# The branch and output projections of an encoder layer, ordered by weights over all three token chunks, with two sets of three banks

## The chip, the cores and the metric

The kernel runs on one core of one Trainium2 chip. The metric is the device time of one execution in microseconds (us).

## The reference

One encoder layer is applied to two groups of tokens, 1024 of `x_sample` and 256 of `x_prompt`, with the same weights and a model width of 1024. Cut to what the change touches:

```
y_a    = o_a   @ w_branch_a          # o_a: 1024 wide (gated linear attention)
y_b    = o_att @ w_branch_b          # o_att: 512 wide (dilated attention)
merged = sigmoid(gate_a) * y_a + sigmoid(gate_b) * y_b
x      = x + merged @ w_out
x      = x + relu(rms_norm(x) @ w_mlp1)**2 @ w_mlp2
x      = x + sigmoid(rms_norm(x) @ w_ple_gate) * (p @ w_ple_proj)
```

Everything before `y_a` (the projection by `w_in` and both attention branches) takes the first half of the kernel and is not changed.

## The kernel before

Activations lie transposed: 128 features on the partitions, 1280 tokens in the free dimension. The tokens are cut into three **chunks** of 512, 512 and 256 (`CHUNKS`, L63), one bank of the matmul accumulator each (a bank holds 512 fp32 values per partition, and there are eight). The precision of fp32 is kept by splitting both operands into a high and a low part, and a product of two tiles is three matmuls (`steps`, L690 to L701): high weights by high activations (L698), high weights by low activations (L699), low weights by high activations (L700). The high parts are made by ScalarE (a copy to the reduced type), the low parts by VectorE (a subtraction).

A **slab** is 128 output features for all tokens. Its weights, KT = 8 tiles of 128 x 128, come by one DMA of SyncE's queue into `w_raw` (`load`), are split by ScalarE (`split_high`, L1029 to L1032) and VectorE (`split_low`, L1373 to L1376, which increments `w_split`) and lie in one of two slots. TensorE computes a slab in `whole` (L703 to L709): for each chunk it waits for the weights and for the chunk's bank to have been read (`ready`, L684 to L688, which asks `evac` for chunk c of the slab before), then for inputs, and runs the 24 products of that chunk (12 where the contraction is only 512 wide), the last of which increments `mm_done`. So a slab uses banks 0, 1 and 2, chunk 0 is complete after two fifths of the slab, and the reader of a bank works while TensorE fills the next.

The change touches two stages. Stage **C1** (L924 to L927) makes `merged`, in eight rounds j of two slabs: slab A (`act_hi`, `act_lo` by `w_branch_a`, 3 x 24 products) and slab B (`ob_hi`, `ob_lo` by `w_branch_b`, 3 x 12 products). Its parts:

- Before it, in the last slab of the input projection, ScalarE evacuates a chunk (L1248) and turns that chunk of the loaded `o_a` into `act_hi` (L1253), VectorE makes `act_lo` (L1641) and increments `c_low`. Chunk c may be overwritten as soon as TensorE is through with it. TensorE's first slab waits for `c_low` per chunk.
- GpSimd waits for all of `merged` of round j-1 (`m_done`, L650) and then loads the two gate rows of round j into rows 16 and 17 of `work` (L653). ScalarE splits the weights of slab B, applies the sigmoid to both rows (L1265), and splits the weights of the next slab A (L1260 to L1266).
- VectorE (`merge_tile`, L1656 to L1675) splits the weights of slab B, waits for the sigmoid (`g_sig`), multiplies the three chunks of slab A into gate row 16 (L1669), splits the weights of the next slab A, and then per chunk of slab B multiplies into row 17 (L1669) and adds both into `merged` (L1673, which increments `m_done`).
- In the last round `merged` must also be split into `act_hi` and `act_lo` for the next stage. ScalarE does it chunk after chunk, eight rows each (L1268 to L1272), the eighth row of a chunk only after VectorE has merged that chunk; VectorE does seven rows of a chunk (L1653), then merges the chunk, then does the eighth, and increments `m_low`. Both engines go through the chunks in this one order.

Stage **C2** (L937 to L949) makes `x + merged @ w_out` in eight slabs. Per chunk TensorE waits for the bank, for `m_low` of that chunk and, at chunk 0, for the rows of x (`xn_loaded`), adds x by products with the identity (L947, ten of 128 columns per slab, each of which shows as two instructions in the trace), then runs the 24 products. ScalarE evacuates the three chunks (L1284), squares the row (L1288), and at the start of the next turn splits weights; VectorE adds up the squares (L1689) and increments `x1_acc`. When the last slab is through, ScalarE and VectorE prepare the inputs of the MLP (`norm_rows`, L1294 and L1695), and column sums of the squares (L933) give the norm.

The MLP stage (L955 to L970), which is not changed, runs `whole` for its first product and for its second one a loop over four banks (3 to 6), with six products into each before it goes to the next.

Of the kernel before, what the change touches and what calls it, by code (L numbers as in the profile page):

```python
# [19 lines left out]
ALU = mybir.AluOpType  # L20
ACT = mybir.ActivationFunctionType
# [4 lines left out]
P = 128  # L26
# [27 lines left out]
def encoder(nc, a, out_p, out_s):  # L54
# [3 lines left out]
    KT = D // P  # L58
# [29 lines left out]
    def slab_chunks(n):  # L88

        return 3 * n  # L90

    with ExitStack() as ctx:
# [590 lines left out]
        def _(pe):  # L683
# [19 lines left out]
            def whole(n, slot, kt, hi, lo, inputs=None):  # L703

                for c in range(3):
                    ready(n, c)
                    if inputs is not None:
                        inputs(c)
                    steps(slot, c, 0, kt, kt, hi, lo).then_inc(mm_done, 1)  # L709


            def transposed_x(c):

                for k in range(KT):
                    q = c * KT + k
                    if k == 0:
                        pe.wait_ge(x_norm, X_TILES[c][1])
                    if q >= 5:
                        pe.wait_ge(x_low, q - 4)
                    for i, t in enumerate(range(*X_TILES[c])):  # L720
                        mm = nc.tensor.transpose(bank[3 + q % 5][:, i * P:i * P + P], x_in[:, t, k * P:k * P + P],
                                                 ident[:])
                    mm.then_inc(x_tr, 1)
# [197 lines left out]
                whole(N_REST + j, (N_REST + j) % 2, KT, act_hi, act_lo)  # L921


            with pe.Fori(0, KT) as j:  # L924
                n = N_C1 + 2 * j
                whole(n, N_C1 % 2, KT, act_hi, act_lo, lambda c: pe.wait_ge(c_low, 8 * c + 9))
                whole(n + 1, (N_C1 + 1) % 2, 4, ob_hi, ob_lo, lambda c: pe.wait_ge(c_low, 24 + 5))  # L927


            def column_sums(row, first, last):  # L930
# [6 lines left out]
            with pe.Fori(0, KT // 2) as i:  # L937
                for e in range(2):
                    n = N_C2 + e + 2 * i
                    xt = x_row(e).rearrange("p (n d) -> p n d", d=P)  # L940
                    for c, (t0, tw) in enumerate(CHUNKS):
                        ready(n, c)
                        pe.wait_ge(m_low, 8 * c + 9)
                        if c == 0:
                            pe.wait_ge(xn_loaded[e], 32 * i + 32)
                        for q in range(tw // P):
                            nc.tensor.matmul(bank[c][:, q * P:q * P + P], xt[:, t0 // P + q, :], ident[:],  # L947
                                             start=q == 0, stop=False, skip_group_check=True)
                        steps((N_C2 + e) % 2, c, 0, KT, KT, act_hi, act_lo, first=False).then_inc(mm_done, 1)  # L949
            pe.wait_ge(head_done, H + 1)  # L950
            pe.wait_ge(x1_acc, KT + 2)
            column_sums(8, True, True).then_inc(x1_ss, 1)

# [71 lines left out]
        def _(act):  # L1025
# [250 lines left out]
            with act.Fori(0, KT // 2) as i:  # L1276
                for e in range(2):
                    n = N_C2 + e + 2 * i
                    split_high(n + 1, (N_C2 + e + 1) % 2)
                    row = work[:, bass.ds(2 * i + e, 1), :].rearrange("p o t -> p (o t)")  # L1280
                    for c, (t0, tw) in enumerate(CHUNKS):
                        act.wait_ge(mm_done, slab_chunks(n) + c + 2)
                        act.sem_inc(act_passed, 1)
                        A(row[:, t0:t0 + tw], bank[c][:, 0:tw], ACT.Copy).then_inc(evac, 1)  # L1284
                    act.wait_ge(evac, slab_chunks(n + 1) + 1)
                    act.wait_ge(x1_acc, 2 * i + e + 1)
                    act.sem_inc(act_passed, 1)
                    A(work[:, 12 + e, :], row, ACT.Square).then_inc(x1_sq, 1)  # L1288
# [80 lines left out]
        def _(dve):  # L1369
# [286 lines left out]
            def merge_tile(j, last):  # L1656
                n = N_C1 + 2 * j
                split_low(n + 1, (N_C1 + 1) % 2, 512)
                for e in range(2):
                    if e == 1:  # L1660
                        split_low(n + 2, N_C1 % 2)
                    dve.wait_ge(g_sig, 2 * j + e + 2)
                    for c, (t0, tw) in enumerate(CHUNKS):
                        if last and e == 1:
                            for k in range(KT - 1):
                                merged_low(c, k)
                        gate = work[:, 16 + e, t0:t0 + tw]
                        chunk_done(n + e, c)
                        v_.tensor_tensor(gate, bank[c][:, 0:tw], gate, ALU.mult).then_inc(evac, 1)  # L1669
                        if e == 1:  # L1670
                            dve.wait_ge(evac, slab_chunks(n + 1) + c + 2)
                            both = merged[:, bass.ds(j, 1), t0:t0 + tw].rearrange("p o t -> p (o t)")
                            v_.tensor_tensor(both, work[:, 16, t0:t0 + tw], gate, ALU.add).then_inc(m_done, 1)  # L1673
                            if last:
                                merged_low(c, KT - 1)  # L1675
# [111 lines left out]
```

## Time and profile before

| | |
|---|---|
| median of 3 runs | 2964.9 us (2960.98, 2964.90, 2965.68) |
| span of the profiled execution | 2963.3 us, from the first to the last instruction |
| time of the profiled execution outside its span | not recorded; the median run is 1.6 us above that span |
| TensorE busy | 2850.8 us (96%), 15390 matmuls and as many weight loads |
| VectorE, ScalarE, GpSimd busy | 1181.4, 991.7, 157.5 us |
| mean granted TensorE clock | 0.982 of full |
| stage C1 in the trace | 1571.9 to 1745.2 us |
| stage C2 in the trace | 1748.0 to 1878.2 us |
| MLP in the trace | 1887.3 to about 2772 us |

Times in the rows are microseconds from the span's start. "PE" is TensorE's matmul, "PEld" its weight load, "DVE" VectorE, "ACT" ScalarE, "POOL" GpSimd. Matmuls overlap in the records: what a product costs is the distance from one start to the next, not its duration. A bracket at the end of a row is the engine's idle time before it and who ended it.

### The profile page before, as it was taken

The numbers are of one execution on the slowest core, as the hardware profiler recorded it, in microseconds if no ns is written. First come the engines' busy times: TensorE is split into PE (matmuls) and PEld (weight loads), VectorE is DVE, ScalarE is ACT, GpSimd is POOL, SyncE is SP. The second block draws the span as 40 slices with busy tenths as digits, with TensorE's granted clock in tenths as the row PEclk, the third lists the DMA queues.
The fourth block names the chain that finished last, engine by engine and source line by source line (L and its number), as shares of the span: only waits on it lengthen the run. The fifth ranks groups of instructions, "written<-read, shape, count | busy, mean of one in ns | idle before, by whom it ended". The sixth has DMA issues, their size and how long they took to land.

```text
span 2963.3 us, 41636 instructions
## 1 busy us (share of the span) xinstructions
PE 2850.8 (96%) x15390; PEld 2433.3 (82%) x15390; DVE 1181.4 (40%) x1917; ACT 991.7 (33%) x1639; POOL 157.5 (5%) x247
## 2 busy tenths in 40 slices
PE   5999999999999899998999999999999999999798
PEld 5887888878888788887887888788888888888687
DVE  3224433334323443235324341454444444544533
ACT  4454225442344423544234332412112112212422
POOL 2001000010000100001010001000000000000000
PEclk8999999989999999999999999999999999999999
DMA  3122121131212211122143222111111111111022
GB/s 95 29 30 43 45 72 31 23 56 31 74 29 30 50 41 64 30 30 59 38 181 119 88 93 73 54 35 42 36 35 42 35 41 37 35 42 35 9 74 59
DMA packets 176579, 153.25 MB, mean 52 GB/s; under 512 B 13745, under 2 KB 155393, under 8 KB 176449
## 3 DMA queue, kind: packets, MB, share of 16 engines
q1 hardware_dynamic: 153824, 94.38, 11.4%
q0 software_dynamic: 16352, 57.00, 7.2%
q8 instruction: 80, 1.31, 0.2%
q10 hardware_dynamic: 6272, 0.15, 0.1%
q14 instruction: 51, 0.41, 0.1%
HBM read 127.48 MB, written 23.78 MB: 51 GB/s over the span
## 4 chain that ended last, share of the span: by engine, by line
PE 87%; DVE 4%; DMA 3%; issue 3%; ACT 2%; POOL 1%; ACTq 0%; DVEq 0%; SPq 0%; POOLq 0%
PE bank L698 25%; PE bank L700 24%; PE bank L699 24%; PE bank L857 2%; PE bank L806 2%; PE bank L787 1%; PE bank L900 1%; PE bank L882 1%; DMA stat_scratch<-st_t 1%; PE bank L897 1%; DMA work<-weight_scratch 1%; DVE work L1524 1%; PE bank L797 1%; PE bank L947 1%; DVE work L1504 1%
## 5 line engine op out<-in xcount | busy, mean ns | idle before, releaser
L698 PE MATMUL bank<-act_hi,w_hi 128*128 128x512 f32 (+1 forms) x3192 | 1189.4, 373 | 47.6 <-ACT work L1232 32.9
L700 PE MATMUL bank<-act_hi,w_lo 128*128 128x512 f32 (+1 forms) x3192 | 1139.0, 357 | 0.0
L699 PE MATMUL bank<-act_lo,w_hi 128*128 128x512 f32 (+1 forms) x3192 | 1138.5, 357 | 0.0
L698 PEld LDWEIGHTS bank<-act_hi,w_hi 128*128 128x128 f32 x3192 | 608.4, 191 | 134.7 <-ACT work L1232 35.2
L700 PEld LDWEIGHTS bank<-act_hi,w_lo 128*128 128x128 f32 x3192 | 607.0, 190 | 89.0
L699 PEld LDWEIGHTS bank<-act_lo,w_hi 128*128 128x128 f32 x3192 | 609.6, 191 | 74.4
L1032 ACT ACTIVATE w_hi<-w_raw 128x1024 fp32r<-128x1024 f32 (+2 forms) x179 | 180.0, 1006 | 437.5 <-PE bank L700 392.3
L1375 DVE TENSOR_TENSOR w_lo<-w_raw,w_hi 128x1024 fp32r<-128x1024 f32 (+2 forms) x181 | 210.8, 1165 | 242.7 <-ACT w_hi L1032 238.0
L698 PE MATMUL bank<-u_hi,w_hi 128*128 128x512 f32 (+1 forms) x816 | 289.6, 355 | 2.4 <-DVE work L1746 2.4
L699 PE MATMUL bank<-u_lo,w_hi 128*128 128x512 f32 (+1 forms) x816 | 289.5, 355 | 0.0
L700 PE MATMUL bank<-u_hi,w_lo 128*128 128x512 f32 (+1 forms) x816 | 289.0, 354 | 0.0
L1723 DVE TENSOR_TENSOR work<-bank,work 128x512 f32<-128x512 f32 (+1 forms) x384 | 226.7, 601 | 136.9 <-PE bank L700 134.0
L1232 ACT ACTIVATE work<-bank 128x512 f32<-128x512 f32 (+1 forms) x216 | 111.8, 524 | 413.5 <-PE bank L700 412.6
L698 PEld LDWEIGHTS bank<-u_hi,w_hi 128*128 128x128 f32 x816 | 154.7, 190 | 24.6 <-DVE w_lo L1375 2.8
L699 PEld LDWEIGHTS bank<-u_lo,w_hi 128*128 128x128 f32 x816 | 154.7, 190 | 21.4
L700 PEld LDWEIGHTS bank<-u_hi,w_lo 128*128 128x128 f32 x816 | 154.5, 189 | 21.6
L1315 ACT ACTIVATE utmp<-utmp 128x512 f32<-128x512 f32 (+1 forms) x96 | 53.8, 561 | 308.8 <-DVE utmp L1711 308.8
L1711 DVE SCALAR_TENSOR_TENSOR utmp<-bank,r_bc 128x512 f32<-128x512 f32 (+1 forms) x96 | 57.8, 602 | 161.5 <-PE bank L700 157.5
L1714 DVE TENSOR_TENSOR u_lo<-utmp,u_hi 128x512 fp32r<-128x512 f32 (+1 forms) x96 | 57.9, 603 | 117.0 <-ACT u_hi L1317 117.0
L1175 ACT ACTIVATE kdn<-bank 128x256 f32<-128x256 f32 x40 | 15.4, 384 | 232.4 <-PE bank L859 232.4
L561 POOL DMA_DIRECT2D stat_scratch<-st_t x48 | 49.4, 1034 | 758.9 <-DVE st_t L1475 725.0
L1442 DVE SCALAR_TENSOR_TENSOR work<-work,g_k 128x1280 f32<-128x1280 f32 x12 | 18.6, 1551 | 148.6 <-ACT work L1111 148.6
(228 smaller groups left out, 2691.7 us busy)
## 6 DMA issues: line engine op xcount, KB each, us to landing
w_raw<-in_w_in_dram SPq DMA_DIRECT2D x76, 512.0 KB, 3.7
w_raw<-in_w_mlp_dram SPq DMA_DIRECT2D x64, 512.0 KB, 3.9
gate_scratch<-work POOLq DMA_DIRECT2D x16, 640.0 KB, 3.2
work<-gate_scratch POOLq DMA_DIRECT2D x16, 640.0 KB, 6.5
work<-weight_scratch POOLq DMA_DIRECT2D x12, 640.0 KB, 5.9
oa_scratch<-work POOLq DMA_DIRECT2D x8, 640.0 KB, 6.0
work<-oa_scratch POOLq DMA_DIRECT2D x8, 640.0 KB, 8.0
x_in<-in_x_sample_dram SPq DMA_DIRECT2D x8, 512.0 KB, 8.0
```

The lines of the kernel that those rows point to most:

```text
L698: nc.tensor.matmul(out, wh, rh, start=first and k == 0, stop=False, skip_group_check=True)
L699: nc.tensor.matmul(out, wh, rl, start=False, stop=False, skip_group_check=True)
L700: mm = nc.tensor.matmul(out, wl, rh, start=False, stop=k == kt - 1, skip_group_check=True)
L806: mm = nc.tensor.matmul(bank[6][:, 0:P], ar[p0:p1, 2, m * P:m * P + P], prt[p0:p1, b % 2, i * P:i * P + P], start=i == 0, stop=i == len(pc ...
L857: nc.tensor.matmul(out, keys_, queries_, start=True, stop=True, skip_group_check=True)
L1032: A(w_hi[:, slot, 0:width], w_raw[:, 0:width], ACT.Copy).then_inc(w_high, 1)
L1232: A(dst, src, ACT.Copy, scale=DK ** -0.5 if tt == 9 else 1.0).then_inc(evac, 1)
L1315: A(buf, buf, ACT.Square).then_inc(u_sq, 1)
L1375: v_.tensor_tensor(w_lo[:, slot, 0:width], w_raw[:, 0:width], w_hi[:, slot, 0:width].bitcast(F32), ALU.subtract).then_inc(w_split, 1)
L1711: v_.scalar_tensor_tensor(out=buf, in0=bank[c][:, 0:tw], scalar=0.0, in1=r_bc[:, t0:t0 + tw], op0=ALU.max, op1=ALU.mult).then_inc(evac, 1)
L1714: v_.tensor_tensor(u_lo[:, e, t0:t0 + tw], buf, u_hi[:, e, t0:t0 + tw].bitcast(F32), ALU.subtract).then_inc(u_low, 1)
L1723: v_.tensor_tensor(x, bank[3 + jt][:, 0:tw], x, ALU.add).then_inc(w2_read if jt < 3 else evac, 1)
```

## The change

`swept` replaces `whole` in stages C1 and C2. It takes the bank set e (banks 0 to 2 or 3 to 5), waits at the slab's start for the weights and for the inputs and banks of all three chunks, and then runs the products with the chunk as the innermost loop: for each of the KT tiles and each of the three pairs of parts, the same 128 x 128 weights for chunks 0, 1 and 2. The number of products, and of weight loads that the program asks for, is the same. The wait for a bank now asks for chunk c of the slab before the last. In C2 the products with the identity for all three chunks come at the slab's start. The last product of each chunk, which increments `mm_done`, is now among the slab's last three. Two waits are added ahead of C1: for the evacuation of all earlier slabs, and for `head_done`, which stood behind C2. The readers (L1284 and L1669) take the bank of the set.

```
--- before.py
+++ after.py
@@ -707,6 +707,26 @@
                     if inputs is not None:
                         inputs(c)
                     steps(slot, c, 0, kt, kt, hi, lo).then_inc(mm_done, 1)
+
+
+            def swept(n, e, slot, kt, hi, lo, inputs, begin=None):
+
+                banks = bank[3 * e:3 * e + 3]
+                pe.wait_ge(w_split, n + 2)
+                for c in range(3):
+                    pe.wait_ge(evac, slab_chunks(n - 2) + c + 2)
+                    inputs(c)
+                    if begin is not None:
+                        begin(c, banks[c])
+                for k in range(kt):
+                    wh, wl = w_hi[:, slot, k * P:k * P + P], w_lo[:, slot, k * P:k * P + P]
+                    for w, x in ((wh, hi), (wh, lo), (wl, hi)):
+                        for c, (t0, tw) in enumerate(CHUNKS):
+                            mm = nc.tensor.matmul(banks[c][:, 0:tw], w, x[:, k, t0:t0 + tw],
+                                                  start=begin is None and k == 0 and w is wh and x is hi,
+                                                  stop=k == kt - 1 and w is wl, skip_group_check=True)
+                            if k == kt - 1 and w is wl:
+                                mm.then_inc(mm_done, 1)
 
 
             def transposed_x(c):
@@ -921,10 +941,12 @@
                 whole(N_REST + j, (N_REST + j) % 2, KT, act_hi, act_lo)
 
 
+            pe.wait_ge(evac, slab_chunks(N_C1) + 1)
+            pe.wait_ge(head_done, H + 1)
             with pe.Fori(0, KT) as j:
                 n = N_C1 + 2 * j
-                whole(n, N_C1 % 2, KT, act_hi, act_lo, lambda c: pe.wait_ge(c_low, 8 * c + 9))
-                whole(n + 1, (N_C1 + 1) % 2, 4, ob_hi, ob_lo, lambda c: pe.wait_ge(c_low, 24 + 5))
+                swept(n, 0, N_C1 % 2, KT, act_hi, act_lo, lambda c: pe.wait_ge(c_low, 8 * c + 9))
+                swept(n + 1, 1, (N_C1 + 1) % 2, 4, ob_hi, ob_lo, lambda c: pe.wait_ge(c_low, 24 + 5))
 
 
             def column_sums(row, first, last):
@@ -938,16 +960,19 @@
                 for e in range(2):
                     n = N_C2 + e + 2 * i
                     xt = x_row(e).rearrange("p (n d) -> p n d", d=P)
-                    for c, (t0, tw) in enumerate(CHUNKS):
-                        ready(n, c)
+
+                    def inputs(c):
                         pe.wait_ge(m_low, 8 * c + 9)
                         if c == 0:
                             pe.wait_ge(xn_loaded[e], 32 * i + 32)
+
+                    def residual(c, out):
+                        t0, tw = CHUNKS[c]
                         for q in range(tw // P):
-                            nc.tensor.matmul(bank[c][:, q * P:q * P + P], xt[:, t0 // P + q, :], ident[:],
+                            nc.tensor.matmul(out[:, q * P:q * P + P], xt[:, t0 // P + q, :], ident[:],
                                              start=q == 0, stop=False, skip_group_check=True)
-                        steps((N_C2 + e) % 2, c, 0, KT, KT, act_hi, act_lo, first=False).then_inc(mm_done, 1)
-            pe.wait_ge(head_done, H + 1)
+
+                    swept(n, e, (N_C2 + e) % 2, KT, act_hi, act_lo, inputs, residual)
             pe.wait_ge(x1_acc, KT + 2)
             column_sums(8, True, True).then_inc(x1_ss, 1)
 
@@ -1281,7 +1306,7 @@
                     for c, (t0, tw) in enumerate(CHUNKS):
                         act.wait_ge(mm_done, slab_chunks(n) + c + 2)
                         act.sem_inc(act_passed, 1)
-                        A(row[:, t0:t0 + tw], bank[c][:, 0:tw], ACT.Copy).then_inc(evac, 1)
+                        A(row[:, t0:t0 + tw], bank[3 * e + c][:, 0:tw], ACT.Copy).then_inc(evac, 1)
                     act.wait_ge(evac, slab_chunks(n + 1) + 1)
                     act.wait_ge(x1_acc, 2 * i + e + 1)
                     act.sem_inc(act_passed, 1)
@@ -1666,7 +1691,7 @@
                                 merged_low(c, k)
                         gate = work[:, 16 + e, t0:t0 + tw]
                         chunk_done(n + e, c)
-                        v_.tensor_tensor(gate, bank[c][:, 0:tw], gate, ALU.mult).then_inc(evac, 1)
+                        v_.tensor_tensor(gate, bank[3 * e + c][:, 0:tw], gate, ALU.mult).then_inc(evac, 1)
                         if e == 1:
                             dve.wait_ge(evac, slab_chunks(n + 1) + c + 2)
                             both = merged[:, bass.ds(j, 1), t0:t0 + tw].rearrange("p o t -> p (o t)")
```

## Rows read from the trace of the kernel before

**Rows 1.** The page's head.
```profile
span 2963.3 us, 41636 instructions
```

**Rows 2.** Busy time by stretch: us, PE, PEld, DVE, ACT, POOL; PEclk, DMA share, GB/s.
```profile
1599.50:1724.70 125.20, 125.20 (x659) 108.09 (x658) 43.92 (x68) 40.17 (x36) 6.38 (x12) 1.00 0.31 101
...
1920.00:2750.00 830.00, 830.00 (x4336) 715.79 (x4335) 394.50 (x604) 161.25 (x240) 0.00 (x0) 1.00 0.13 39
```

**Rows 3.** What TensorE waited for, 1550 to 1920 us: us, times, longest.
```profile
PE bank L698 <- DVE work L1669: 5.5, 1, 5.5
PE bank L933 <- DVE work L1689: 3.8, 1, 3.8
PE bank L947 <- DVE act_lo L1653: 2.6, 1, 2.6
```

**Rows 4.** The groups by line and form, one of the weight loads.
```profile
L699 PEld LDWEIGHTS bank<-act_lo,w_hi 128*128 128x128 f32 x3192 | 609.6, 191 | 74.4
```

**Rows 5.** Timeline of PE, two slabs: start, duration, engine, line, operation, count.
```profile
1558.16 0.40 PE L698 MATMUL bank<-act_hi,w_hi 128*128 128x512 f32 x1
...
1569.06 0.28 PE L698 MATMUL bank<-act_hi,w_hi 128*128 128x256 f32 x1
...
1571.94 0.40 PE L698 MATMUL bank<-act_hi,w_hi 128*128 128x512 f32 x1
...
1600.48 0.40 PE L698 MATMUL bank<-act_hi,w_hi 128*128 128x512 f32 x1
...
1600.94 0.39 PE L700 MATMUL bank<-act_hi,w_lo 128*128 128x512 f32 x1
```

**Rows 6.** Timeline, start of C1 and the first slab B.
```profile
1570.41 7.59 DVE L1641 TENSOR_TENSOR act_lo<-work,act_hi 128x512 fp32r<-128x512 f32 x16 [0.53 <-ACT act_hi L1253]
...
1585.60 0.28 PE L700 MATMUL bank<-act_hi,w_lo 128*128 128x256 f32 x1
...
1591.34 0.80 PE L698 MATMUL bank<-ob_hi,w_hi 128*128 128x512 f32 x1 [5.47 <-DVE work L1669]
...
1596.08 0.39 PE L700 MATMUL bank<-ob_hi,w_lo 128*128 128x512 f32 x1
```

**Rows 7.** Timeline, end of round 6 of C1 and the sigmoid of round 7.
```profile
1723.32 0.69 DVE L1669 TENSOR_TENSOR work<-bank,work 128x512 f32<-128x512 f32 x1 [1.08 <-PE bank L700]
...
1724.56 0.40 PE L698 MATMUL bank<-act_hi,w_hi 128*128 128x512 f32 x1
...
1724.77 0.41 DVE L1669 TENSOR_TENSOR work<-bank,work 128x256 f32<-128x256 f32 x1
1725.32 0.42 DVE L1673 TENSOR_TENSOR work<-work 128x256 f32 x1
...
1734.02 2.44 ACT L1265 ACTIVATE work<-work 128x1280 f32<-128x1280 f32 x2 [7.33 <-DMA work<-gate_scratch]
```

**Rows 8.** Timeline, the passage from C1 to C2 and C2's first two slabs.
```profile
1739.63 1.23 DVE L1375 TENSOR_TENSOR w_lo<-w_raw,w_hi 128x1024 fp32r<-128x1024 f32 x1 [0.67 <-ACT w_hi L1032]
...
1745.12 0.28 PE L700 MATMUL bank<-ob_hi,w_lo 128*128 128x256 f32 x1
...
1748.03 1.15 PE L947 MATMUL bank<-ident,x_next 128*128 128x128 f32 x8 [2.63 <-DVE act_lo L1653]
...
1758.33 0.42 DVE L1653 TENSOR_TENSOR act_lo<-work,act_hi 128x256 fp32r<-128x256 f32 x1 [0.48 <-ACT act_hi L1272]
...
1765.74 1.06 PE L947 MATMUL bank<-ident,work 128*128 128x128 f32 x8
...
1781.78 0.61 PE L947 MATMUL bank<-ident,x_next 128*128 128x128 f32 x4
```

**Rows 9.** Timeline of ACT, the end of C2.
```profile
1875.10 0.60 ACT L1284 ACTIVATE work<-bank 128x512 f32 x1 [5.75 <-PE bank L700]
1878.42 0.38 ACT L1284 ACTIVATE work<-bank 128x256 f32 x1 [2.72 <-PE bank L700]
...
1880.17 13.10 ACT L1294 ACTIVATE act_hi<-work,g_mlp 128x512 fp32r<-128x512 f32 x24
```

## The prediction

> **What bounds the kernel now.** I read the page's head for the span [rows 1], then the busy time by stretch [rows 2], then TensorE's list of waits around the two stages [rows 3], and last the timeline at each border. The stretches show that TensorE is the bound: inside stage C1 it is busy for all of 125.2 us at a granted clock of 1.00, while DVE works 43.9 and ACT 40.2 us [rows 2]. So a change there can pay in two ways only: a product must become cheaper, or one of TensorE's few waits must go. The list holds 5.5, 3.8 and 2.6 us [rows 3], each once.
>
> A product's price is the distance between starts. 48 products of 512 columns took 1558.16 to 1569.06, 0.2271 us each, and the next 24 of 256 columns 2.88 us, 0.120 us each [rows 5]. The difference, 0.107 us for 256 columns, is the streaming at the 2.4 GHz level; 0.013 us per product is fixed. Slab A is then 48 x 0.227 + 24 x 0.120 = 13.78 us, slab B 6.89, a round 20.67. A slab of C2 takes 16.04 (1765.74 to 1781.78) [rows 8].
>
> **Does the order by weights make a product cheaper?** I take no gain. The program before already repeats weights: L699 uses the weights of L698, and yet has its own load, 3192 of them at 191 ns [rows 4], and 0.227 us is the mean over all three lines, with no room for one of them to be 0.013 cheaper unless another is dearer. The loads lie beside the products. Nor does changing the bank show a price or a gain: the 24 products of 256 columns from 1569.06 include the step into bank 0 at 1571.94 [rows 5], and the MLP stage, which changes bank every six products, is busy for all of 830 us [rows 2].
>
> The Trainium skill (TensorE: Matmul & The Clock Gate, Step-by-step: what each phase is for) says that weights are loaded apart so that they can be loaded once and used for many products. By that the order would save the loads; no row here shows a load that is left out.
>
> What the new order does add is a step from 256 back to 512 columns in every group of three. Nearest rows: the first two products of 512 after a run of 256 took 1600.48 to 1600.94, 0.46 where two of 0.227 make 0.454 [rows 5]. That is 0.006 us per group, with the rounding 0 to 0.016. Groups: 8 rounds x 36 + 8 slabs x 24 = 480. I take +2.9 us, ends 0 and +7.7. The identity products of C2 only move together; the count is the same, and I cost that at nothing.
>
> **Start of C1.** Now all of `act_lo` must be there before the first product. VectorE ends it at 1570.41 + 7.59 = 1578.00 [rows 6]; with 0.2 us from a finish to its reader (TensorE through at 1724.56, VectorE starts 1724.77 [rows 7]) TensorE starts at 1578.2 instead of 1571.94: +6.26. The second set of banks takes away one wait: slab B of round 0 stood from 1585.60 + 0.12 = 1585.72 to 1591.34 for the late gates, 5.62 us [rows 6]. Slab B now needs banks 3 to 5, which are free, so -5.62, and slab A's banks are wanted only a slab later. TensorE was slow after that stand: 1591.34 to 1596.08 for 11 products, 4.74 against 2.50, a loss of 2.24 us [rows 6]. The new stand is as long, so the loss moves with it. Net **+0.64**, and C1 ends at 1745.24 + 0.64 = 1745.88.
>
> **Rounds of C1.** All three chunks of slab B now end together, so VectorE's merge comes behind the slab: pairs of 1.45, 1.45 and 0.97 us (1723.32 to 1724.77, and 1724.77 to 1725.32 + 0.42 [rows 7]), 3.87 with 0.21 ahead. `merged` is done 4.1 us after slab B where it was 1725.74 - 1724.56 = 1.2. GpSimd's gate load and ACT's sigmoid are queued behind it: the sigmoid starts 8.28 us after `merged` (1725.74 to 1734.02) and takes 2.44. Then come ACT's and VectorE's weight splits, 1.1 and 1.2 us. Sum 4.1 + 8.28 + 2.44 + 1.1 + 1.2 = 17.1 us into a round in which the next slab A starts at 20.67. So 3.5 us are left, and I cost this at nothing. The cover is slab B; without it each round would lose what is over.
>
> **From C1 to C2, the main term.** Before, TensorE worked on chunks 1 and 2 of the last slab and then on chunk 0 of C2 while ScalarE and VectorE split `merged` chunk by chunk; it stood only 2.63 us, and the last low part was done at 1758.33 + 0.42 = 1758.75, hidden under C2's first slab [rows 8]. Now the first slab's products need all of it. The chain also starts later. Round 6 ends at 1724.56 + 0.64 = 1725.2, `merged` is done 4.1 later (1729.3), the sigmoid starts at 1737.6 and ends at 1740.0, and the low weights follow 1.1 later, at 1741.1, where they came at 1739.63. From there to the last low part it was 19.12 us of ScalarE and VectorE in a fixed order, which I keep: 1760.2. With 0.2 to wake and 0.45 for chunk 2's identity products (a quarter of 8 + 8 + 4 instructions, the others run during the wait), the products start at 1760.9. The engine has stood for most of 14 us, so I add 2.24 for the slow clock (as after 5.6 us; the first slab of before lost 1765.74 - 1748.03 - 16.04 = 1.67; ends 1.7 and 3.4). The slab ends at 1760.9 + 13.78 + 2.24 = 1776.9, where before it was 1765.74. That is **+11.2**, the 0.64 within it.
>
> **C2 and its end.** The banks of the slab before the last are always free, the rows of x and the weights are asked for after a whole slab as before, with 16 us for them: nothing. At the end ScalarE finds three chunks to evacuate where one was left (1878.42; a copy of 512 takes 0.60 [rows 9]). Two more, back to back, are **+1.15**, and the square, the 13.10 us of `act_hi` for the MLP and all behind it follow ScalarE [rows 9]. The MLP itself is as it was.
>
> **Sum.** 11.2 + 1.15 + 2.9 = +15.2 us on the profiled span of 2963.3, so 2978.5; on the median of the runs, 1.6 above that span, 2980.1, or 0.5% slower. About 0.2%, 6 us, is what a measurement of this kernel can tell from no change.
>
> **Rivals.** (1) *The fixed 0.013 us goes.* It could be the price of writing the same bank twice running, or of changing weights. `swept` never writes a bank twice running: 1440 products x 0.0129 = 18.6 us against 12.35 of stalls and evacuation, -6.2: 2958.7. If only products whose weights repeat gain (7 of 9, 1120), it is 14.4: 2962.8. It decides from 8.6 ns per product on. Against it stand the equal spacings across a change of bank and on L699 [rows 4, 5]; for it, only that no row has both at every product. Chance 0.07, half of it faster. (2) *The clock falls in the interleaved slabs.* A product at the low level cost 2.24 / 11 = 0.204 us more [rows 6]; one in ten of 1440 would be 29 us: 3009. Against: granted 1.00 through 830 us of changing banks [rows 2]. Chance 0.03.
>
> The Trainium skill has a rule that speaks for this rival (TensorE: Matmul & The Clock Gate, A second HAM failure mode: psum-queue depth-cycling): cycling through banks lets TensorE idle in small gaps often enough that its clock goes up and down. In the MLP stage of this trace that doesn't happen.
>
> (3) *The gates come too late in C1*, with 3.5 us left. If each load were 5.5 us slower beside the weights' load, seven rounds would lose 2 each: +14, 2994. The margin speaks against it. Chance 0.04. (4) *The passage is cheaper than I read*, ScalarE and VectorE being done sooner because nothing else holds them: half the term, 2974 to 2971. Chance 0.06.
>
> **Numbers.** My own case has 0.80, and 2973 to 2987 by its ends: groups of three -2.9 to +4.8, the clock -0.5 to +1.2, the chain 1.5 either way, the runs' spread 2.5 either way. The range that leaves out no more than two in ten takes in rival 4 and some of rival 1: 2969 to 2988. Within 0.2% I put 0.08 (half of rival 1, some of rival 4), faster 0.04, slower 0.88.
>
> **What would show it.** TensorE's first C1 product near 1578 and no stand at slab B of round 0; then a stand ahead of C2's products of some 14 us, broken only by the first sixteen identity instructions, released by L1653; groups of three every 0.574 to 0.59 us; three evacuations back to back behind each slab of C2; as many weight loads as before, 15390. It would be wrong if the groups took under 0.56 us, if TensorE waited in the rounds of C1, or if the stand ahead of C2 were under 8 us.

## Result and profile after

The changed kernel takes 2983.16 us in the median of 4 runs (2982.60 to 2986.05) where the kernel before took 2965.29 (2960.98 to 2971.72): a ratio of 1.0061, 95% interval 1.0046 to 1.0075, +17.9 us. The forecast was 2980.1, in a range of 2969 to 2988, slower with a chance of 0.88. The sign and the mechanism were as forecast; one term of the sum was put at half of what it measured.

The head of the page and TensorE's list of waits from 1550 to 1920 us (us in total, times, longest), which answer to [rows 1] and [rows 3]:

```profile
span 2984.3 us, 41636 instructions
```
```profile
PE bank L972 <- DVE act_lo L1678: 10.8, 3, 5.7
PE bank L725 <- DVE act_lo L1666: 6.0, 1, 6.0
PE bank L955 <- DVE work L1714: 4.3, 1, 4.3
```

The wait for late gates (5.5 us) is gone, 6.0 us ahead of C1 and 10.8 us ahead of C2 have come (L725 is the product in `swept`, L972 the identity product, L1666 and L1678 the low parts). The timeline of TensorE at the start of C1, against [rows 6]; x3 is one group of three products:

```profile
1574.67 0.28 PE L700 MATMUL bank<-act_hi,w_lo 128*128 128x256 f32 x1
1580.99 1.41 PE L725 MATMUL bank<-act_hi,w_hi 128*128 128x512 f32 x3 [6.05 <-DVE act_lo L1666]
...
1586.96 0.74 PE L725 MATMUL bank<-act_hi,w_hi 128*128 128x512 f32 x3
```

TensorE stands (waits, without work) from 1574.67 + 0.12 to 1580.99, 6.20 us. The six groups that follow take 5.97 us where six at full clock take 3.52: 2.45 us for the 1.2 GHz level. The granted clock bears it out (busy time by stretch, columns as in [rows 2]; the clock is the third number from the end):

```profile
1581.00:1586.00 5.00, 5.00 (x14) 4.13 (x15) 3.69 (x3) 4.97 (x5) 2.74 (x4) 0.50 0.53 156
1750.00:1780.00 30.00, 19.24 (x91) 16.18 (x90) 16.67 (x30) 9.37 (x20) 1.61 (x2) 0.77 0.19 55
```

The second row holds the passage to C2, with a granted clock of 0.77 on the mean. Then the groups inside C1, against [rows 5], and the passage to C2, against [rows 8] (two engines' timelines):

```profile
1639.75 0.75 PE L725 MATMUL bank<-ob_hi,w_hi 128*128 128x512 f32 x3
...
1641.51 0.75 PE L725 MATMUL bank<-ob_hi,w_hi 128*128 128x512 f32 x3
...
1751.81 0.74 PE L725 MATMUL bank<-ob_hi,w_lo 128*128 128x512 f32 x3
1755.64 1.15 PE L972 MATMUL bank<-ident,x_next 128*128 128x128 f32 x8 [3.09 <-DVE act_lo L1678]
1762.47 2.05 PE L972 MATMUL bank<-ident,x_next 128*128 128x128 f32 x8 [5.67 <-DVE act_lo L1678]
1766.51 1.19 PE L972 MATMUL bank<-ident,x_next 128*128 128x128 f32 x4 [2.00 <-DVE act_lo L1678]
1767.36 1.20 PE L725 MATMUL bank<-act_hi,w_hi 128*128 128x512 f32 x2
...
1782.98 1.28 PE L972 MATMUL bank<-ident,work 128*128 128x128 f32 x10
```
```profile
1734.67 0.42 DVE L1698 TENSOR_TENSOR work<-work 128x256 f32 x1
...
1747.24 1.23 DVE L1400 TENSOR_TENSOR w_lo<-w_raw,w_hi 128x1024 fp32r<-128x1024 f32 x1 [0.36 <-ACT w_hi L1057]
...
1765.94 0.43 DVE L1678 TENSOR_TENSOR act_lo<-work,act_hi 128x256 fp32r<-128x256 f32 x1 [0.48 <-ACT act_hi L1297]
```

Three groups take 1.76 us, 0.587 each, where three products of the kernel before take 0.574. The last slab of C1 ends at 1752.4 and the first products of C2 come at 1767.36: 15 us, broken only by the identity products, and ended by the last low part at 1765.94 + 0.43. VectorE's chain from the weights (1747.24) to there takes 19.1 us, as before. The loads of weights are as many as before, 15390 on either page; this is one of the groups by line and form, with [rows 4]:

```profile
L725 PEld LDWEIGHTS bank<-act_lo,w_hi 128*128 128x128 f32 x384 | 64.8, 191 | 11.6
```

### Where a trace is late

The two profiled spans differ by 21.0 us, of which 2.85 lie ahead of C1, in code that is the same in both. Since the kernels issue the same number of matmuls (e7's 74 added ones are left out), the k-th one of each trace can be set against the k-th of the kernel before. This table, worked out from the traces, gives how much later it starts than before, less the difference that was already there at the border of C1. Its last column comes within 2.7 us of every timed difference. Each row is one execution. Two pairs of kernels have the same code in C1, the changed one and e2, and the kernel before and e3; in the first column they differ by 0.57 and 0.70 us. So a difference of under 1 us between two rows says nothing. The table is still finer than the timing, whose intervals are 5 to 9 us wide.

```
us late at:             C1's end  C2 slab 1  C2's end  column sums  MLP
(time in before)         1745.12   1765.74    1877.94   1882.00     1910
changed kernel             +4.30    +14.39     +16.16    +16.70   +17.85
e1 slab B, own banks       -6.70     -6.68      -6.68     -6.68    -6.70
e2 swept in C1             +3.73     +3.83      +3.83     +3.83    +3.80
e3 swept in C2             -0.70     +8.79     +10.56    +11.09   +12.20
e4 weights rotated         +3.67    +13.17     +14.95    +15.48   +15.59
e5 two chunks and one      +1.19    +10.91     +10.82    +10.73   +10.84
e6 tile by tile            +2.34    +11.25     +12.05    +12.10   +12.19
e7 waits filled            +1.92     +9.79     +11.56    +12.09   +12.16
e8 borders by chunk        -3.69     -4.36      -2.84     -2.93    -2.87
e9 two sets, by chunk      -6.50     -8.60      -8.61     -8.61    -8.64
e10 large and small        +2.40    +13.10     +13.98    +14.52   +14.59
e11 one set, swept        +52.17    +63.39     +69.99    +70.53   +70.61
```

For the changed kernel: +4.3 in C1, +10.1 in the passage and C2's first slab, +1.8 in the other seven slabs, +0.5 for the end of C2 and +1.15 from there into the MLP, 17.85 in all, and 17.9 timed.

### The profile page after: what moved, and what is told of

The parts are those of the page before. It is cut to its first block, busy times and chain, and to the rows that moved or that the text cites. A ratio compares the mean times of both kernels' runs of the same rounds, so it can differ in the third digit from the quotient of the medians.

```text
span 2984.3 us, 41636 instructions
## 1 busy us (share of the span) xinstructions
PE 2861.3 (96%) x15390; PEld 2438.4 (82%) x15390; DVE 1180.0 (40%) x1917; ACT 989.5 (33%) x1639; POOL 157.6 (5%) x247
## 4 chain that ended last, share of the span: by engine, by line
PE 87%; DVE 4%; DMA 3%; issue 3%; ACT 1%; POOL 1%; ACTq 0%; DVEq 0%; SPq 0%; POOLq 0%
PE bank L698 22%; PE bank L700 21%; PE bank L699 21%; PE bank L725 9%; PE bank L877 2%; PE bank L826 2%; PE bank L807 1%; DMA stat_scratch<-st_t 1%; PE bank L920 1%; PE bank L902 1%; PE bank L917 1%; DMA work<-weight_scratch 1%; DVE work L1549 1%; PE bank L817 1%; DVE work L1529 1%
## 5 line engine op out<-in xcount | busy, mean ns | idle before, releaser
L698 PE MATMUL bank<-act_hi,w_hi 128*128 128x512 f32 (+1 forms) x2808 | 1052.0, 375 | 49.0 <-ACT work L1257 34.8
L699 PE MATMUL bank<-act_lo,w_hi 128*128 128x512 f32 (+1 forms) x2808 | 1003.9, 358 | 0.0
L700 PE MATMUL bank<-act_hi,w_lo 128*128 128x512 f32 (+1 forms) x2808 | 1003.8, 357 | 0.0
L698 PEld LDWEIGHTS bank<-act_hi,w_hi 128*128 128x128 f32 x2808 | 536.4, 191 | 126.4 <-ACT work L1257 36.7
L700 PEld LDWEIGHTS bank<-act_hi,w_lo 128*128 128x128 f32 x2808 | 535.1, 191 | 79.0
L699 PEld LDWEIGHTS bank<-act_lo,w_hi 128*128 128x128 f32 x2808 | 537.4, 191 | 64.7
L1748 DVE TENSOR_TENSOR work<-bank,work 128x512 f32<-128x512 f32 (+1 forms) x384 | 226.7, 601 | 136.9 <-PE bank L700 134.0
L725 PE MATMUL bank<-act_hi,w_hi 128*128 128x512 f32 (+1 forms) x384 | 98.1, 364 | 6.0 <-DVE act_lo L1666 6.0
L725 PE MATMUL bank<-act_lo,w_hi 128*128 128x512 f32 (+1 forms) x384 | 97.1, 362 | 0.0
L725 PE MATMUL bank<-act_hi,w_lo 128*128 128x512 f32 (+1 forms) x384 | 96.6, 360 | 0.0
```

The costliest lines, as they stand in the source:

```text
L698: nc.tensor.matmul(out, wh, rh, start=first and k == 0, stop=False, skip_group_check=True)
L699: nc.tensor.matmul(out, wh, rl, start=False, stop=False, skip_group_check=True)
L700: mm = nc.tensor.matmul(out, wl, rh, start=False, stop=k == kt - 1, skip_group_check=True)
L725: mm = nc.tensor.matmul(banks[c][:, 0:tw], w, x[:, k, t0:t0 + tw], start=begin is None and k == 0 and w is wh and x is hi, stop=k == kt - ...
L1748: v_.tensor_tensor(x, bank[3 + jt][:, 0:tw], x, ALU.add).then_inc(w2_read if jt < 3 else evac, 1)
```

## The experiments

The timed ones, each against the kernel before on the same chip:

```
                       us      before    ratio    95% interval
e1_banks            2963.88   2969.91   0.9980   0.9971 to 0.9989
e2_swept_c1         2974.75   2969.91   1.0016   1.0006 to 1.0025
e3_swept_c2         2981.84   2969.91   1.0038   1.0025 to 1.0051
e8_borders          2969.01   2969.91   1.0001   0.9991 to 1.0010
e7_filled           2982.66   2968.62   1.0046   1.0032 to 1.0060
e9_sets_by_chunk    2962.10   2970.52   0.9973   0.9964 to 0.9982
one run each: e4_no_repeat 2985.52, e5_two_and_one 2980.59, e6_by_tile 2980.91 (before 2968.62);
              e10_large_small 2987.74, e11_one_set 3042.22 (before 2970.52)
```

### The second set of banks alone

On the kernel before, slab B alone moves (in C1, TensorE and VectorE; the wait for `head_done` moves ahead of C1 too, and TensorE doesn't stand there):

```
+            def other_set(n, slot, kt, hi, lo, inputs):
+                pe.wait_ge(w_split, n + 2)
+                for c, (t0, tw) in enumerate(CHUNKS):
+                    pe.wait_ge(evac, slab_chunks(n - 2) + c + 2)
+                    inputs(c)
+                    steps(slot, c, 0, kt, kt, hi, lo, out=bank[3 + c][:, 0:tw]).then_inc(mm_done, 1)
...
-                whole(n + 1, (N_C1 + 1) % 2, 4, ob_hi, ob_lo, lambda c: pe.wait_ge(c_low, 24 + 5))
+                other_set(n + 1, (N_C1 + 1) % 2, 4, ob_hi, ob_lo, lambda c: pe.wait_ge(c_low, 24 + 5))
...
-                        v_.tensor_tensor(gate, bank[c][:, 0:tw], gate, ALU.mult)
+                        v_.tensor_tensor(gate, bank[3 * e + c][:, 0:tw], gate, ALU.mult)
```

> The kernel before, with one part of the change alone: slab B of stage C1 goes to banks 3 to 5, all slabs stay chunk by chunk. Theory (the loss comes from handing all three chunks over at once, and the second set of banks is a gain by itself): slab B of round 0 doesn't stand for the gates, so its 5.6 us and the 2.24 us of slow clock behind it go, and nothing takes their place: 7.9 us less than before, some 2957 us; the distance between products stays 227 and 120 ns. Rival (two sets of banks cost something themselves, by changing banks or by later evacuation): no gain, or slower by some us.

It is 6.0 us faster, 6.7 by the table. The timeline of TensorE, ahead of round 1:

```profile
1599.73 0.28 PE L700 MATMUL bank<-ob_hi,w_lo 128*128 128x256 f32 x1
1600.62 0.50 PE L698 MATMUL bank<-act_hi,w_hi 128*128 128x512 f32 x1 [0.62 <-DVE work L1678]
```

Of the 7.9 us expected, one came back here: slab A of round 1 is still in banks 0 to 2 and asks for slab B's first evacuation, which the late gates hold up. The rival falls: slab B in its own banks costs nothing and brings 6 us.

### The order by weights in one stage at a time

The changed kernel with the other stage as it was before:

```
 e2:  C1 swept, two sets;  C2 chunk by chunk in banks 0 to 2
 e3:  C1 chunk by chunk in banks 0 to 2;  C2 swept, two sets
```

> The changed kernel with stage C2 as before (chunk by chunk, banks 0 to 2). Theory: the start of C1 and its 288 groups of three at 0.5867 us instead of 0.574 put C1's end 4.4 us late (6.2 + 2.45 - 5.6 - 2.24 + 3.6), C2 starts on chunk 0 as before and so follows at +4.8: some 2970 us. Rival (the last slab of C1 being swept is what delays C2): most of the 17.9 us is here, 2980.

> The changed kernel with stage C1 as before (chunk by chunk, banks 0 to 2). Theory: C2's first slab waits for the low parts of all chunks, ready at about 1758.8 us in the time of the trace before, so its products start 11 us late, its end is 9.3 late, 168 groups more add 2.1 us and the last three evacuations 1.15: +12.5, some 2978 us. Rival: under +5, with the passage bound by C1's last slab.

Measured +4.8 and +11.9 us, +3.8 and +12.2 by the table. So the passage is paid for by how C2 begins and not by how C1's last slab ends: with C2 chunk by chunk, C1's lateness is handed on unchanged (+3.73 to +3.83). With C2 swept, TensorE waits for the same three low parts as in the changed kernel (timeline of e3):

```profile
1751.81 1.15 PE L971 MATMUL bank<-ident,x_next 128*128 128x128 f32 x8 [2.63 <-DVE act_lo L1677]
1758.64 2.05 PE L971 MATMUL bank<-ident,x_next 128*128 128x128 f32 x8 [5.67 <-DVE act_lo L1677]
1762.68 1.20 PE L971 MATMUL bank<-ident,x_next 128*128 128x128 f32 x4 [2.00 <-DVE act_lo L1677]
```

### The order by weights kept, the borders by chunk

`chunked` has the arguments of `swept` and its two sets of banks, but waits and multiplies per chunk, as `whole` does; `pair` issues slabs A and B of a round, `out_pair` two slabs of C2.

```
+            pair(0, chunked, swept, back=1)
+            with pe.Fori(1, KT - 1) as j:
+                pair(j, swept, swept)
+            pair(KT - 1, chunked, chunked)
...
+            out_pair(0, (chunked, swept))
+            with pe.Fori(1, KT // 2 - 1) as i:
+                out_pair(i, (swept, swept))
+            out_pair(KT // 2 - 1, (swept, chunked))
```

> The changed kernel, order by weights kept inside the stages (372 groups of three), but the slabs at the borders chunk by chunk: slab A of round 0, both slabs of the last round, the first and the last slab of C2. Theory (borders make the loss): the 14 us stand ahead of C2 and the 6 us one ahead of C1 are gone; 372 groups cost 4.7 us, the freed wait for the gates gives 7.9, the later sigmoid of the last round takes 1.5: some 1.7 us less than before, 2963. Rival (the order by weights is itself what costs, in every slab): still 10 us or more above before, 2975.

A ratio of 1.0001, so no difference from before; by the table -2.9, of which 372 groups of three are some +4.7 (12.6 ns each, as worked out below). The rival falls: 372 of the 480 groups are still swept, and 18 us of the loss are gone (20.7 by the table). In the passage the wait for chunk 0 is left, and 0.22 us for chunk 1 (timeline):

```profile
1750.32 1.13 PE L989 MATMUL bank<-ident,x_next 128*128 128x128 f32 x8 [3.08 <-DVE act_lo L1700]
1757.14 1.13 PE L989 MATMUL bank<-ident,x_next 128*128 128x128 f32 x8 [0.22 <-DVE act_lo L1700]
```

### What a group of three pays for

Four orders of the same products, all on the changed kernel:

```
 e4:  for s in 0..2: for c in 0..2:  pair (s + c) % 3 of (wh, hi), (wl, hi), (wh, lo), chunk c
 e5:  all tiles of chunks 0 and 1 interleaved, then chunk 2 alone
 e6:  per tile: three products of chunk 0, three of chunk 1, three of chunk 2
 e10: chunk 1 alone, then all tiles of chunks 0 and 2 interleaved
```

> The changed kernel, the chunk still innermost (512, 512, 256 columns, a new bank each time), but the three pairs of parts rotated against the chunks, so that most neighbouring products have other weights (wh, wl, wh; wl, wh, wh; wh, wh, wl). Theory (repeating weights is worth nothing and costs nothing; the 12.6 ns more per group come from the steps between sizes or banks): a group keeps its 0.587 us. Rival (repeated weights are the cheaper or the dearer thing): the group moves by 5 ns or more, to 0.574 or to 0.60.

> The changed kernel, with chunks 0 and 1 interleaved (two banks, both 512 columns, weights used twice running) and chunk 2 after them alone. Theory (the step in size costs, not the change of bank): products of 512 come every 227 ns and those of 256 every 120. Rival (each change of bank costs): products of 512 come every 229 to 233 ns.

> The changed kernel, tile by tile: for each 128 x 128 tile, three products of chunk 0, three of chunk 1, three of chunk 2. So sizes and banks change every three products and not every one. Theory (each step in size costs some ns, one time): nine products take 1.722 us + 12.6 ns, as against 1.760 us in the changed kernel. Rival (a step disturbs the next two or three products as well): nearer to 1.75 us.

> The changed kernel, chunk 1 alone first and then chunks 0 and 2 interleaved: one step down and one step up in size for every two products (a large, a small). Theory (the price is per visit to the 256-column chunk, 12.6 ns, as in the groups of three): a pair takes 347 + 12.6 = some 360 ns, the 512s of chunk 1 alone 227. Rival (the price belongs to the two large products that follow one another after a small one): a pair takes 347 to 353 ns.

The timelines of TensorE in e4, e5 and e6, inside C1:

```profile
1640.35 0.39 PE L729 MATMUL bank<-act_hi,w_hi 128*128 128x512 f32 x1
1640.58 0.40 PE L729 MATMUL bank<-act_hi,w_lo 128*128 128x512 f32 x1
1640.82 0.28 PE L729 MATMUL bank<-act_lo,w_hi 128*128 128x256 f32 x1
1640.94 0.39 PE L729 MATMUL bank<-act_hi,w_lo 128*128 128x512 f32 x1
...
1641.53 0.39 PE L729 MATMUL bank<-act_lo,w_hi 128*128 128x512 f32 x1
```
```profile
1642.99 0.62 PE L729 MATMUL bank<-ob_hi,w_hi 128*128 128x512 f32 x2
1643.45 0.61 PE L729 MATMUL bank<-ob_lo,w_hi 128*128 128x512 f32 x2
1643.90 0.62 PE L729 MATMUL bank<-ob_hi,w_lo 128*128 128x512 f32 x2
1644.35 0.62 PE L729 MATMUL bank<-ob_hi,w_hi 128*128 128x512 f32 x2
```
```profile
1640.46 0.40 PE L729 MATMUL bank<-ob_hi,w_hi 128*128 128x512 f32 x1
...
1641.85 0.28 PE L729 MATMUL bank<-ob_hi,w_hi 128*128 128x256 f32 x1
...
1642.20 0.40 PE L729 MATMUL bank<-ob_hi,w_hi 128*128 128x512 f32 x1
```

e4: a group is 0.59 us with a third of the neighbours sharing weights instead of seven in nine; the mean over 100 groups of the trace is 587 ns in both kernels. Repeating weights, with a load issued for each product all the same, is worth nothing and costs nothing. e5: two banks in turn, the high weights used four times running and the low ones twice, and a pair takes 0.453, exactly two products of the kernel before. So changing the bank costs nothing either; what costs is the small product between large ones. e6: nine products take 1.74 us where they took 1.722 before and take 1.760 in the changed kernel, +18 and +38 ns. My theory of 12.6 ns per visit to the small chunk gave +12.6 there and was too low: the first five large products after the small ones take 233, 236, 228, 233 and 230 ns in the trace, 27 ns more than five of 226.7, and the first small one is 7 short (113). The kernel before pays the same at the start of each slab (234, 235, 229, 232, 231 ns behind a run of small ones).

In e10 large and small products alternate (timeline):

```profile
1640.32 0.51 PE L730 MATMUL bank<-act_hi,w_hi 128*128 128x512 f32 x2
1640.67 0.51 PE L730 MATMUL bank<-act_lo,w_hi 128*128 128x512 f32 x2
1641.02 0.53 PE L730 MATMUL bank<-act_hi,w_lo 128*128 128x512 f32 x2
1641.38 0.51 PE L730 MATMUL bank<-act_hi,w_hi 128*128 128x512 f32 x2
```

Three pairs take 1.06 us, 0.353 each against 0.347 for one product of either size: some 6 ns, not 12.6, at the upper end of the rival's 347 to 353. So the price isn't one per visit; it depends on how many large products follow. Against products far from any step in size (226.7 and 120.0 ns in the traces) a return to the large size costs 6.7 ns with one large product behind it (e10), 13.3 with two (the changed kernel) and 20 with six (e6); the mean of before, to which 6, 12.6 and 18 refer, has one return per slab in it. Why, no run here says. Its total in the changed kernel is 480 x 12.6 ns = 6.0 us, and e5, which returns to the large size once a slab like the kernel before, is 5.3 us less late at C2's end (10.82 against 16.16).

### The clock behind the stands

```
+            def fill(count, moving):
+                for _ in range(count):
+                    nc.tensor.matmul(bank[6][:, :], ones_r[:], moving, start=True, stop=True, skip_group_check=True)
...
+            pe.wait_ge(c_low, 9)
+            fill(24, act_hi[:, 0, 0:512])
...
+            fill(50, ob_hi[:, 0, 0:512])
```

> The changed kernel, with 24 products of 512 columns into an idle bank (results unused) while TensorE waits ahead of C1, and 50 while it waits ahead of C2. Theory (the stands cost their own length and then 2.45 and 1.54 us of products at the 1.2 GHz level): the clock stays granted, and the time is 3 to 4 us less than the changed kernel's, at 14 us above before (some 2984 where before is 2970). Rival (the slow clock is not worth that, or the added products delay the real ones): no difference from the changed kernel, 18 us above before.

```profile
1578.18 5.63 PE L715 MATMUL bank<-act_hi,ones_r 128*128 128x512 f32 x24
1584.39 0.81 PE L730 MATMUL bank<-act_hi,w_hi 128*128 128x512 f32 x3 [0.58 <-DVE act_lo L1674]
...
1753.41 11.54 PE L715 MATMUL bank<-ob_hi,ones_r 128*128 128x512 f32 x50
1764.78 1.95 PE L980 MATMUL bank<-ident,x_next 128*128 128x128 f32 x16
```

The real groups come at full speed from the second product on, and the granted clock is 1.00 in the stretch where it was 0.77 (busy time by stretch):

```profile
1750.00:1780.00 30.00, 29.54 (x152) 25.00 (x151) 17.34 (x31) 9.99 (x21) 1.61 (x2) 1.00 0.20 57
```

It is 14.0 us above before, as expected, but the intervals of the two kernels overlap, so the timing alone doesn't decide; the table does: at C1's end it is 2.4 us less late than the changed kernel (1.92 against 4.30), through the passage another 2.2. That is 4.6 us for the slow clock, where I had read 3.99 from the rows; the 0.6 between them is within what two traces differ by.

### Sweeping on one set of banks

```
-                banks = bank[3 * e:3 * e + 3]
+                banks = bank[0:3]
-                    pe.wait_ge(evac, slab_chunks(n - 2) + c + 2)
+                    pe.wait_ge(evac, slab_chunks(n - 1) + c + 2)
```

> The changed kernel on one set of banks: slabs swept as in the change, all in banks 0 to 2, so each slab waits for the evacuation of the one before. Theory (with all chunks handed over together, evacuation can't lie beside products unless there is a second set): slab B stands some 1.9 us and slab A 3.6 us in each round, C2's slabs 1.6 us each, some 50 us more than the changed kernel, about 3035. Rival (evacuation is short enough to matter little): under 15 us more.

```profile
1669.19 0.85 PE L725 MATMUL bank<-act_hi,w_hi 128*128 128x512 f32 x3 [3.16 <-DVE work L1694]
1686.40 0.85 PE L725 MATMUL bank<-ob_hi,w_hi 128*128 128x512 f32 x3 [1.36 <-DVE work L1694]
1696.84 1.07 PE L725 MATMUL bank<-act_hi,w_hi 128*128 128x512 f32 x3 [3.15 <-DVE work L1694]
```

52.8 us more late than the changed kernel by the table (70.61 - 17.85), where some 50 were forecast. The split was not as forecast: 47.9 us of it lie in C1, where the stands expected make 8 x 5.5 = 44, and 4.9 behind it, where they make 8 x 1.6 = 12.8. A round takes 27.65 us (1669.19 to 1696.84) where 36 groups of 0.587 take 21.1; 4.5 of the 6.5 us are the two waits of the rows, and the groups behind the longer one are slow (1.07 us for the slowest).

### The version that beats both

The kernel before on two sets in both stages, every slab chunk by chunk; in C2 the identity products come ahead of the waits for the low parts:

```
+                    for c, (t0, tw) in enumerate(CHUNKS):
+                        pe.wait_ge(evac, slab_chunks(n - 2) + c + 2)
+                        for q in range(tw // P):
+                            nc.tensor.matmul(bank[3 * e + c][:, q * P:q * P + P], xt[:, t0 // P + q, :], ident[:],
+                                             start=q == 0, stop=False, skip_group_check=True)
+                    pe.wait_ge(w_split, n + 2)
+                    for c, (t0, tw) in enumerate(CHUNKS):
+                        pe.wait_ge(m_low, 8 * c + 9)
+                        steps((N_C2 + e) % 2, c, 0, KT, KT, act_hi, act_lo, out=bank[3 * e + c][:, 0:tw],
+                              first=False).then_inc(mm_done, 1)
```

> The kernel before with both stages on two sets of banks, every slab chunk by chunk. In C2 the identity products of all three chunks come first, ahead of the waits for the low parts, which are still per chunk. Theory (two sets are the useful part of the change): C1 gains the 6.7 us that its trace showed with slab B in banks 3 to 5; in C2's first slab the identity products (2.2 us) run inside the 2.6 us that TensorE waits for chunk 0, so another 1.3 us (those of chunk 0 were the only ones behind that wait, the others only move) to 3 us with the clock kept up. Together 8 to 9.5 us less than before. Rival (in C2 the second set is worth nothing, and all identity products at once hold up the first chunk): no more than the 6 us of slab B alone.

```profile
1745.37 2.40 PE L954 MATMUL bank<-ident,x_next 128*128 128x128 f32 x20
1748.07 0.47 PE L698 MATMUL bank<-act_hi,w_hi 128*128 128x512 f32 x1 [0.30 <-DVE act_lo L1664]
1754.91 0.50 PE L698 MATMUL bank<-act_hi,w_hi 128*128 128x512 f32 x1 [1.16 <-DVE act_lo L1664]
```

8.4 us faster than before (ratio 0.9973, interval 0.9964 to 0.9982), and by the table 26.5 us ahead of the changed kernel (17.85 + 8.64). 2.1 us of the gain come between C1's end and C2's second slab (-6.50 to -8.60 in one trace): all 20 identity instructions now fill the wait of [rows 8], and the wait is down to 0.3 us. C2's second set makes room for them; which part it has in the 2.1 us and which the order of the waits, no run separates. The 1.16 us ahead of chunk 1 are new: TensorE is now early enough to find VectorE's chain. The rival, no more than the 6 us of slab B alone, falls by the table (-8.64 against -6.70); the timed intervals of the two overlap.

## Why the prediction was right

**Start of C1.** The step gave a stand of 6.26 and a net of +0.64. The stand was 6.20 and the slow clock behind it 2.45 instead of 2.24, so the net was 6.20 + 2.45 - 5.62 - 2.24 = +0.79. With 288 groups at 12.6 ns, 3.6 us, this makes 4.4 for C1, and the table has 4.3. e1 shows that the wait for the gates was really the set of banks' to take away.

**Groups of three.** This is the term that was mis-sized: +2.9 us, read from the first two products behind a run of small ones (0.006 us), where it is 12.6 ns and 6.0 us, inside the ends of 0 and 7.7 that were given. The two rows gave 0.46 us for the two large products, at two decimals (the trace has 234 and 235 ns, 0.469), and said nothing of the small one. In the changed kernel the trace has 229 and 233 ns for the large ones and 124 for the small one, where it was 227, 227 and 120. That neither weights nor banks have a price was right (e4, e5).

**Rounds of C1.** Nothing was to be lost and nothing was: no wait stands in the list inside the rounds. `merged` of round 6 was done at 1734.67 + 0.42, and the next weights at 1747.24 + 1.23 = 1748.5, 3.9 us ahead of the end of slab B at 1752.4, where the sum left 3.5.

**The passage.** +10.56 was forecast behind C1's end, +10.1 measured, and 0.3 of these are the slab's own groups of three. Stand (15.0 us by the sum, 1767.36 - 1752.40 = 14.96) and chain (19.12, and 19.1) were near; the slow clock was less than taken (2.24, and 15.62 - 14.08 = 1.54). e3 shows that the cause is C2's wait for all chunks, e8 that by chunk it disappears.

**The end of C2.** +1.15 was forecast; the column sums came 0.5 later and the MLP another 1.15. The first was too high, because chunk 0 and 1 end two and one products ahead of chunk 2 and their evacuation begins early. In the trace the three take 1.36 us and begin 0.13 us after the start of the slab's last product, where the one that was left began 0.48 after it (1877.94 to 1878.42). The second I hadn't seen: the sum has the MLP as it was. TensorE stood 4.3 us ahead of the column sums and the MLP's first slab then ran at the low level (products 0.43 apart), where before it was over by then:

```profile
1901.55 4.64 PE L955 MATMUL bank<-work,ones_r 128*128 128x512 f32 x6 [4.32 <-DVE work L1714]
1906.94 0.76 PE L698 MATMUL bank<-act_hi,w_hi 128*128 128x512 f32 x1 [0.76 <-DVE act_lo L1720]
...
1907.93 0.63 PE L700 MATMUL bank<-act_hi,w_lo 128*128 128x512 f32 x1
1908.36 0.63 PE L698 MATMUL bank<-act_hi,w_hi 128*128 128x512 f32 x1
```

e3 has it too (+11.09 to +12.20); e4, e7 and e11, whose TensorE stands as long there, have not (+15.48 to +15.59 in e4). So it doesn't follow from the stand alone. With one trace of each kernel, what decides it stays open.

**The sum.** It was 2.6 us short (15.25 against 17.85). The groups were 3.1 too low and the MLP's slow start of 1.15 was missing, 4.3 together; the passage and the three evacuations were put 0.8 and 0.6 too high and hid part of it, and the rest is less than two traces differ by. So the forecast came nearer than its terms did, by luck. The case's own upper end was also added up wrongly: +4.8, +1.2, +1.5 and +2.5 make 2990, not 2987, and half of the passage gives rival 4 its 2974, but not its 2971. The 2983.2 measured lies within either.

**The rivals.** That the fixed 13 ns goes is out: the changed kernel has both of its conditions and a group got dearer, 0.587 for 0.574; e4 takes away most of the repeats of weights and e5 the small product between the large ones, and in neither do products of 512 columns come less than 0.227 us apart on the mean. That the clock falls inside the stages is out: it was granted in full through the rounds, with a new bank at every product, as the busy time by stretch shows (columns as in [rows 2]):

```profile
1590.00:1720.00 130.00, 130.00 (x666) 110.34 (x665) 41.66 (x66) 39.61 (x36) 6.38 (x12) 1.00 0.30 97
```

The gates didn't come too late in C1, and the passage wasn't cheaper than read.

The rule that was weighed against the change, that cycling through banks makes the clock go up and down (the Trainium skill, TensorE: Matmul & The Clock Gate, A second HAM failure mode: psum-queue depth-cycling), doesn't show in this kernel: the row above has 1.00 for 130 us. The one that spoke for it, that weights once loaded can serve many products (the Trainium skill, TensorE: Matmul & The Clock Gate, Step-by-step: what each phase is for), is not tested by any run here: the program issues a load with each product, and each shows in the trace.

## What to carry to other kernels

When a slab's inputs and results are handed over piece by piece, an order that makes all pieces start and end together saves nothing by itself and must buy back, at each border of a stage, the chain that lay under the pieces: here 10 us at one border. Look for what a change brings besides its aim: the second set of banks, needed only to make the order bearable, was the useful part. Without the order it is worth 6 us for slab B alone, and 8 us in both stages with the identity products moved ahead of the waits. Before an order is changed for cheaper weights, look whether neighbours that share weights are already cheaper.

## What was unexpected of the hardware

At full clock a product of 256 columns between products of 512 makes those that follow it slower: 6.7 ns for each pair of 512, 256, 13.3 ns for each group of 512, 512, 256, 20 ns for nine in threes (6, 12.6 and 18 above the mean of the kernel before). Which weights the neighbours have makes no difference (e4), and two of 512 in turn in two banks pay nothing (e5); but every step in size here is also a step to another bank. At the 1.2 GHz level the price is absent, and so are the fixed 13 ns: in the changed kernel's first groups of C1 the three products take 427, 427 and 213 ns, 1.067 us in all, which is 1280 columns at 1.2 GHz. The cause stays open.
